# Three blocks of 2048 channels on one core: attention heads with split weight units, the bias table's place in the queue, and norms from sums of the last product

## The reference

```python
# block 1: a convolution, gated linear attention, attention over a memory (4 heads)
x = x + y @ w_out;  x = rmsnorm(x, final_g)
# block 2
h = rms_norm(x, norm1_g);  q, k, v, qi, ki, wi, u_s, v_s, ga, gb = split(h @ w_in)
attn = sparse_attention(...)     # 16 heads, top-64 mask, relative bias rel_bias
x = x + (sigmoid(ga) * attn + sigmoid(gb) * sgu) @ w_out
x = x + square(relu(rms_norm(x, norm2_g) @ w_ff1)) @ w_ff2;  x = rms_norm(x, final_g_2)
# block 3
h = rms_norm_3(x, g_pre);  out = (gated MLA attention, 8 heads, and an RWKV scan)(h) @ w_out
x = x + rms_norm_3(out, g_post)
# rmsnorm(x, g) = x * rsqrt(mean(x*x over channels) + 1e-6) * g
```

## Time and profile before

| | |
|---|---|
| median of 3 runs | 4388.12 us (4385.96 to 4388.28) |
| the profiled execution's own time | 4383.17 us |
| its span | 4381.4 us |
| granted TensorE clock, mean | 0.956 |
| TensorE busy | 3999.8 us (91%) |
| VectorE busy | 2473.3 us (56%) |
| ScalarE busy | 1763.0 us (40%) |
| DMA queue of SP | 634.65 MB, 41.9% of 16 engines |

### The profile page before, as it was taken

How to read it: one execution, slowest core, us unless ns; L and a number is a source line. 1 busy time by engine, 2 the same in 40 slices (tenths; PEclk the granted TensorE clock), 3 DMA queues, 4 the chain that set the end, 5 groups by cost and what they waited for, 6 DMA issues and landing times. The chain is left out here.

```text
span 4381.4 us, 87595 instructions
## 1 busy us (share of the span) xinstructions
PE 3999.8 (91%) x36434; PEld 3884.3 (89%) x36434; DVE 2473.3 (56%) x3418; ACT 1763.0 (40%) x2232; POOL 0.2 (0%) x4
## 2 busy tenths in 40 slices
PE   7999989989898899787799999999899899988898
PEld 7999989889888899776798999999899788888788
DVE  4788765965545544435555555454546655565454
ACT  3434343344444433333344444343344333344543
POOL 0000000000000000000000000000000000000000
PEclk9999999999999998898899999999999999999999
DMA  4545444335444453423354555555554211134343
GB/s 178 173 169 183 154 141 158 112 128 179 148 154 154 160 183 127 153 77 136 115 192 155 182 183 182 183 182 183 171 181 145 107 41 41 41 111 130 137 164 135
DMA packets 99246, 638.54 MB, mean 146 GB/s; under 512 B 11136, under 2 KB 14592, under 8 KB 28224
## 3 DMA queue, kind: packets, MB, share of 16 engines
q1 hardware_dynamic: 98976, 634.65, 41.9%
HBM read 626.18 MB, written 8.42 MB: 145 GB/s over the span
## 5 line engine op out<-in xcount | busy, mean ns | idle before, releaser
L252 PE MATMUL ps_gemm<-arena_r,w_hi 128*128 128x256 f32 x16576 | 2224.3, 287 | 117.9 <-ACT w_hi L193 57.2
L252 PEld LDWEIGHTS ps_gemm<-arena_r,w_hi 128*128 128x128 f32 x16576 | 2107.6, 195 | 139.4 <-issue 72.6
L199 DVE TENSOR_TENSOR ring_r<-ring,w_hi 128x1024 fp32r<-128x1024 f32 (+3 forms) x1264 | 1416.4, 1125 | 1206.7 <-ACT w_hi L193 1194.2
L193 ACT ACTIVATE w_hi<-ring 128x1024 fp32r<-128x1024 f32 (+3 forms) x1264 | 1229.2, 978 | 1323.1 <-PE ps_gemm L252 1061.2
L252 PE MATMUL ps_gemm<-arena_r,ring_r 128*128 128x256 f32 x8288 | 1197.4, 286 | 47.5 <-DVE ring_r L199 46.7
L252 PEld LDWEIGHTS ps_gemm<-arena_r,ring_r 128*128 128x128 f32 x8288 | 1086.9, 194 | 58.1 <-DVE ring_r L199 55.5
L249 PE MATMUL ps_gemm<-w_hi,arena_r 128*128 128x256 f32 (+1 forms) x1408 | 193.3, 288 | 1.0 <-ACT w_hi L193 0.9
L1051 DVE SCALAR_TENSOR_TENSOR arena<-arena,vecs (+15 forms) x480 | 192.1, 462 | 0.0
L249 PEld LDWEIGHTS ps_gemm<-w_hi,arena_r 128*128 128x128 f32 x1408 | 183.0, 198 | 3.0 <-ACT w_hi L193 1.9
L394 ACT ACTIVATE arena<-ps_gemm 128x512 f32 (+2 forms) x99 | 59.1, 597 | 247.9 <-PE ps_gemm L252 190.7
L415 ACT ACTIVATE act_tmp<-ps_gemm 128x512 f32<-128x512 f32 x70 | 41.7, 596 | 158.2 <-PE ps_gemm L252 158.1
(11 more groups left out here) (311 smaller groups left out, 2345.7 us busy)
## 6 DMA issues: line engine op xcount, KB each, us to landing
ring<-in_ff SPq DMA_DIRECT2D x128, 1024.0 KB, 5.2
ring<-in_w_out SPq DMA_DIRECT2D x48, 1024.0 KB, 5.1
ring<-in_gate SPq DMA_DIRECT2D x32, 1024.0 KB, 5.0
ring<-in_conv_a SPq DMA_DIRECT2D x16, 1024.0 KB, 5.1
ring<-in_conv_b SPq DMA_DIRECT2D x16, 1024.0 KB, 5.0
ring<-in_gla_v SPq DMA_DIRECT2D x16, 1024.0 KB, 5.0
ring<-in_conv_z SPq DMA_DIRECT2D x16, 1024.0 KB, 5.0
ring<-in_conv_out SPq DMA_DIRECT2D x16, 1024.0 KB, 5.0
```

The lines of the kernel that those rows point to most:

```text
L193: nc.scalar.activation(w_hi[q % 2][:, 0:size], ring[slot][:, part], ACT.Copy).then_inc(hi_ready, 1)
L199: nc.vector.tensor_tensor(ring_lo[slot][:, part], ring[slot][:, part], w_hi[q % 2][:, 0:size].bitcast(F32), ALU.subtract).then_inc(lo_read ...
L252: mm = nc.tensor.matmul(bank[0:cw, 0:T], w[:, k * cols + c * cw:k * cols + (c + 1) * cw], r[:, kk, :], start=start, stop=stop)
```

## The change

Four edits. (1) `attention`: the quarters of the side product are spread over half heads (`cut`): TensorE does one share before the transposes and one between them and the output product; ScalarE and VectorE follow by parts; on VectorE the output of the head before, then the next maximum, come after the scaling and before the remainders. (2) In the top-k stage SP issues the bias copies before the weight loads. (3) The last product of blocks 1 and 2 also sums squares weighted with the squared gain (`gain`), so both norms' sums are known; `norm_twice` makes both roots from them and multiplies by the product of both gains in one step. The inner norm's `mid` is made from unit 2 to 5 of the first product. (4) In `norm_twice` SP runs the stage's loads first, then stores `mid`.

```diff
@@ Prod.pe, Prod.dve_split, Prod.dve (when sums is set)
-                    for c in range(2):
-                        mm = nc.tensor.matmul(psa[:, 0, 0:T], ones[:, :], stat[:, c, :], start=c == 0, stop=c == 1)
+                    for k in range(2 if s.gain else 1):
+                        for c in range(2):
+                            mm = nc.tensor.matmul(psa[:, k, 0:T], ones[:, :], stat[:, 2 * k + c, :], start=c == 0, stop=c == 1)
...
+                    if s.gain:
+                        for c in range(2):
+                            k = 2 * i2 + (2 * j + c)
+                            nc.vector.scalar_tensor_tensor(out=stat[:, 2 + c, :], in0=s.sums[:, bass.ds(k, 1), :].rearrange("p a t -> p (a t)"),
+                                                           scalar=small[:, bass.ds(k + 40, 1)], in1=stat[:, 2 + c, :], op0=ALU.mult, op1=ALU.add)
                     nc.vector.tensor_tensor(total, total, s.chunks(s.sums, i2, j), ALU.add).then_inc(squares_added, 1)
...
+                    if s.gain:
+                        g = vecs[:, VEC_AT[s.gain]:VEC_AT[s.gain] + DC]
+                        nc.vector.tensor_tensor(small[:, 40:40 + DC], g, g, ALU.mult)
+                        nc.vector.memset(stat[:, 2:4, :], 0.0)
@@ norm_twice
+            def make(dve, q):
+                for c in range(4 * q, 4 * q + 4):
+                    x = nc.vector.scalar_tensor_tensor(out=dst[:, c, :], in0=src[:, c, :], scalar=both[:, c:c + 1], in1=outer, op0=ALU.mult, op1=ALU.mult)
+                return x
...
                 def _(sp):
+                    run.sp(sp)
                     for q in range(4):
                         sp.wait_ge(normed, b_norm + q + 1)
                         sp.dma_start(spill[:, 4 * q:4 * q + 4, :], mid[:, 4 * q:4 * q + 4, :]).then_inc(spilled, 16)
-                    run.sp(sp)
                     sp.wait_ge(spilled, 64)
...
-                    root(act, b_in + 1)
-                    for q in range(4):
-                        act.wait_ge(normed, b_norm + q + 1)
-                        nc.scalar.activation(scratch[:, 4 * q:4 * q + 4, :], mid[:, 4 * q:4 * q + 4, :], ACT.Square).then_inc(sq_ready, 1)
-                    root(act, b_in + 2)
+                    root(act, b_in + 1, outer)
                     parts.act(act)
+                    root(act, b_in + 2, inner)
                     run.act(act)
...
-                    for c in range(DC):
-                        pe.wait_ge(sq_ready, b_sq + c // 4 + 1)
-                        mm = nc.tensor.matmul(psa[:, 1, 0:T], ones[:, :], scratch[:, c, :], start=c == 0, stop=c == DC - 1)
...
+                    link(v.tensor_tensor(both, vecs[:, VEC_AT[gain1]:VEC_AT[gain1] + DC], vecs[:, VEC_AT[gain2]:VEC_AT[gain2] + DC], ALU.mult))
+                    dve.wait_ge(sums_done, b_sums)
+                    link(v.tensor_scalar(inner, psa[:, 0, 0:T], 1.0 / D, EPS, ALU.mult, ALU.add))
+                    link(v.tensor_scalar(stat[:, 2, :], inner, EPS, None, ALU.mult))
+                    v.scalar_tensor_tensor(out=outer, in0=psa[:, 1, 0:T], scalar=1.0 / D, in1=stat[:, 2, :], op0=ALU.mult, op1=ALU.add).then_inc(root_in, 2)
+                    dve.wait_ge(root_done, b_root + 1)
+                    link(v.reciprocal(outer, outer))
+                    parts.dve(dve)
+                    lead.dve_unit(dve, 0)
+                    dve.wait_ge(root_done, b_root + 2)
+                    link(v.reciprocal(inner, inner))
+                    lead.dve_unit(dve, 1)
+                    for u in range(2, lead.n):
+                        if u < 6:
+                            for c in range(4 * u - 8, 4 * u - 4):
+                                x = v.scalar_tensor_tensor(out=mid[:, c, :], in0=src[:, c, :], scalar=vcol(gain1, c), in1=inner, op0=ALU.mult, op1=ALU.mult)
                             x.then_inc(normed, 1)
-                    parts.dve(dve)
-                    run.dve(dve)
+                        lead.dve_unit(dve, u)
@@ attention (pe, dve, act)
-            share = [range(h * m // nh, (h + 1) * m // nh) for h in range(nh)]
+            cut = [4 * m * h // (2 * nh) for h in range(2 * nh + 1)]
+            def beside(quarter, eng, h, half):
+                for n in range(cut[2 * h + half], cut[2 * h + half + 1]):
+                    quarter(eng, n // 4, n % 4)
...
-                        for u in share[h]:
-                            side.pe_unit(pe, u)
+                        if side:
+                            beside(side.pe_quarter, pe, h, 0)
                         pe.wait_ge(p_done, h + 1)
...
                         mm.then_inc(tr_done, 1)
+                        if side:
+                            beside(side.pe_quarter, pe, h, 1)
                         pe.wait_ge(trc_done, h + 1)
...
                     for h in range(nh):
-                        if h + 1 < nh:
-                            maximum(h + 1)
                         b = 8 + 4 * (h % 2)
...
                         x.then_inc(p_done, 1)
-                        for u in share[h]:
-                            side.dve_unit(dve, u)
-                        dve.wait_ge(o_done, h + 1)
...
                         if h:
+                            output(h - 1)
+                        if h + 1 < nh:
+                            maximum(h + 1)
+                        for half in range(2 if side else 0):
+                            beside(side.dve_part, dve, h, half)
+                        if gate is not None and h:
                             remainder(h - 1)
+                    output(nh - 1)
...
-                        for u in share[h]:
-                            side.act_unit(act, u)
+                        if side:
+                            beside(side.act_part, act, h, 0)
                         act.wait_ge(tr_done, h + 1)
...
+                        if side:
+                            beside(side.act_part, act, h, 1)
@@ sparse_attention, sync engine
-                    side.sp(sp)
                     sp.wait_ge(act_b, 1)
...
                         sp.dma_start(RBv[k], src).then_inc(dma_b, 16)
+                    side.sp(sp)
                     sp.wait_ge(dma_b, 48)
```

More of the change, by code:

```diff
@@ L231, in pe_body, with body @@
             r_hi, r_lo = rhs
-            def body(i2, j):
+            def body(i2, j, quarters=range(4)):
                 slot = (g0 + j) % 2
-                pe.wait_ge(bank_free, i2 + (g0 + j + 1))
-                for q in range(4):
+                if 0 in quarters:
+                    pe.wait_ge(bank_free, i2 + (g0 + j + 1))
+                for q in quarters:
                     ring_slot, part, _, n = quarter_of(g0 + j, q)
@@ L266, in build, with __init__ @@
         class Prod:
-            def __init__(s, name, rhs, kind, dst=None, src=None, bias=None, scale=1.0, natural=False, at=0, after=False, rows=P, step=2, split=None, needs_loads=False, sums=None, also=None, before=None):
+            def __init__(s, name, rhs, kind, dst=None, src=None, bias=None, scale=1.0, natural=False, at=0, after=False, rows=P, step=2, split=None, needs_loads=False, sums=None, also=None, before=None, gain=None):
                 s.g0 = st.unit
@@ L802, in layer_norm_silu, with norm_twice @@
             counts(4, 1, 1, 1 + side.n, count[0], side.n)
-        def norm_twice(src, gain1, mid, spill, dst, gain2, scratch, split, then, **kw):
+        def norm_twice(src, gain1, mid, spill, dst, gain2, split, then, **kw):
             _, b_sums, b_in, b_root, b_chain, b_norm = norm_base
-            b_sq = norm_base[0]
             count = [0]
-            parts = make_split(mid, dst, DC, gain2, split)
+            both = small[:, 0:DC]
+            inner, outer = stat[:, 1, :], stat[:, 3, :]
+            def make(dve, q):
+                for c in range(4 * q, 4 * q + 4):
+                    x = nc.vector.scalar_tensor_tensor(out=dst[:, c, :], in0=src[:, c, :], scalar=both[:, c:c + 1], in1=outer, op0=ALU.mult, op1=ALU.mult)
+                return x
+            part = lambda buf: (lambda q: buf[:, 4 * q:4 * q + 4, :])
+            parts = Split(4, make, part(dst), part(split[0]), part(split[1]))
             run = Run(*then, **kw)
-            run.prods[0].fresh = by_quarter(parts.split0 + 4, 4)
+            lead = run.prods[0]
+            lead.fresh = by_quarter(parts.split0 + 4, 4)
             (spilled,) = stage_sems("spilled")
@@ L957, in _, with output @@
                             link(nc.vector.tensor_tensor(x, x, sig, ALU.mult))
+                    def output(h):
+                        dve.wait_ge(o_done, h + 1)
+                        if gate is None:
+                            nc.vector.tensor_copy(o(h), psa[:, 3, 0:T]).then_inc(oc_done, 1)
+                        else:
+                            nc.vector.tensor_tensor(o(h), psa[:, 3, 0:T], gate[2](h), ALU.mult).then_inc(oc_done, 1)
                     for h in range(nh):
[L959 to L960 removed]
                         b = 8 + 4 * (h % 2)
@@ L1115, in block_1 @@
```

(4 more changed lines are left out.)

22 lines of the change are left out of this document (8 added, 14 removed).

## The result

The changed kernel takes **4269.23 us** (median of 4 runs, 4265.84 to 4271.06) against 4387.25 (4385.96 to 4388.28) for the kernel before on the same chip: a ratio of 0.973, 95% interval 0.9713 to 0.9747. The profiled execution took 4270.07 us, its span 4268.3.

A forecast was written before the change was run, and what follows sets the result against it. TensorE was taken to set the end almost everywhere, gains lying where it stands still. Terms -53 -10.2 -13.9 -12.9 -24.9 +16.0 = -98.9 us gave 4284 from the profiled 4383.17, 4289 against the median 4388.12; range 4270 to 4312.

The forecast's parts named there:

- Attention, block 2: Block 2's attention stage: quarters around the transposes remove both waits, 9.2 us a head, 151 against 204 us, 53 us less.
- the bound of 57: Block 2's attention: the most it could gain, 57 us, if the overlap of pieces counted end to end is full.
- Blocks 1 and 3: Attention of blocks 1 and 3: the copy's wait goes, 10.2 us (7 to 12) and 13.9 us (11 to 15) less.
- Bias order: End of the top-k stage: bias copies leave earlier, so TensorE starts 12.9 us sooner (12 to 13.2).
- Norms and stores: Between blocks, twice: shorter norm chains give 24.9 us (22 to 27), late-landing residual stores cost 16.0 (8.6 to 18.6).
- my two ends for the stores: Ends of the block entries: stores land 4.3 us late if sharing without loss, 9.3 us late if in a row.
- nearer the second, but the fixed part once: Ends of the block entries: stores nearly in a row with loads, fixed part counted once, 8.0 us late each.
- the free stores (1): Ends of the block entries: the stores cost nothing, 115 us less in all, 4273 us; 9 in 100.
- the unfilled halves (2): Attention: about 1.4 us of the copy's wait stays in each of 28 heads, +39, 4328 us; 8 in 100.
- the queue of VectorE's remainders (3): Attention: remainders behind two TensorE waits make every half pay 2.5 us, +140, slower at 4429 us; 2 in 100.
- the unchanged order (4): Attention: new loops leave TensorE's order as it is, the norms alone changed, 22 us less, 4366 us; 1 in 100.
- all the marks named for the forecast: Profile after: even heads, clock over 0.95, norm 11 to 13 us, no copy or bias waits, two 10 to 12 us waits.

The follow-up runs named there:

- e12: The changed kernel run once more, unaltered, on another chip: 4269.22 us.
- e1: The changed kernel with the attention loop of before (whole units, VectorE's old order), the rest as changed: 4358.08 us.
- e2: The changed kernel with SP's bias copies behind the weight loads again: 4288.33 us.
- e3: The changed kernel with the two norms between blocks, the sums and the place of the residual's stores as before: 4288.76 us.
- e4: The changed kernel with SP issuing the residual's four stores right after the weight loads of the block's first product: 4257.18 us.
- e5: The changed kernel with the residual's four stores issued from GpSimd's own queue as each quarter is made: 4257.77 us.
- e10: The changed kernel with the residual's stores right after the lead product's loads in block 3 only, last in block 2: 4259.97 us.
- e11: The kernel before with one edit, SP issuing the residual's stores after all loads of the stage: 4405.79 us against 4386.53.
- e13 to e15: The changed kernel with an added stage of 2, 5 or 8 VectorE clears ahead of the RWKV stage: 4271.68, 4271.34 and 4277.52 us.
- e7: The changed kernel with the same quarters per head, but all ahead of the transposes and none after: 4320.7 us.
- e9: The changed kernel with the residual's stores right after the lead product's loads in block 2 only, last in block 3: 4260.3 us.

## Why the prediction was wrong, step by step

Against the profiled execution the forecast was 98.9 us less, and 113.1 came. Two steps failed: the forecast put the stages that the change does not touch at nothing, without a reason, and they gave 10.1 us; and its head of block 2's attention was 0.44 us too long, which made that term 6.1 us too small. Either alone would have left the time inside the range. The missing 14.2 is 10.1 and 6.1, 0.3 each for block 3's attention and the bias order, 0.5 for norms and stores, 1.8 for the last stretch, less 5.0 at the start. With the stretches of the table:

- **Untouched stages: nothing forecast, 10.1 measured** (RWKV stage 7.9, the one before it 2.2). **This is the larger of the two steps that failed.** The forecast had no term for it and its range no room: I took stages that keep their code to keep their time. What decides between about 409 and 417 us was settled in part. Shown: the changed kernel has 409 in both of its profiles (e12); attention does not bring it about (e1); undoing the bias order or the norms takes it away (e2, e3), and so does moving the stores in both blocks (e4, e5). Some 4.6 to 4.8 us of the difference lie in the first 100 us and go with the places of the low clock stretches there; in the changed kernel one of them falls ahead of the wait for VectorE and costs nothing. The rest, 0.8 to 3.4 us, and all 4.1 us of e10, come later, with a stop of TensorE of 1 to 2 us and with further low stretches. Open is what puts a kernel into one form or the other, and what makes the stop. The pause at block 3's entry alone does not decide it (e11), nor does a start up to 6 us later (e13 to e15).
- **Attention, block 2: 53 forecast, 59.1 measured. This is the other step that failed.** The mechanism was right (idle time gone, clock 0.99, no wait left), the term was mis-sized. I put a head together as 0.60 + 2.86 + 5.76 = 9.2 us; it takes 8.78. From the start of one piece to the next it is 0.36 for the transposes, 2.95 and 3.07 for the quarters and 2.40 for the output product and scores. The 2.86 ran to the modelled end of the last scores, 1856.05, though a TensorE record's end lies beyond the start of the next: in e7, after the same wait, the next quarter starts 2.50 us after the output product (1833.63 to 1836.13). The transposes were 0.24 us too long in the same way and the quarters 0.26 too short. So 0.44 us too much in 16 heads, 7 us, less 1 us because 4.4 us of the stage's 144.9 lie outside the 16 heads and not 3.5. I had named the overlap, as the bound of 57, and even that was short.
- **Blocks 1 and 3: 10.2 and 13.9 forecast, 10.2 and 14.2 measured** (e1: 9.9 and 14.3). e7, which takes away nothing there but the cover behind the transposes, gives 9.9 and 15.6 back.
- **Bias order: 12.9 forecast, 13.2 measured**, and 13.2 again in e2. Its weight loads behind the copies cost nothing, as said.
- **Norms and stores: 24.9 - 16.0 forecast, 9.4 net measured for 8.9.** From the sum product on, the chains gave 12.6 and 13.1 us (12.45 each forecast). The forecast's chain starts one step earlier and counts the two multiply-adds, which are there (3.43 us ahead of the sum product for 2.64); like for like it is 11.8 and 12.3. The items of its chain also add up to 11.3 us and not to the 11.5 it states. The stage ends lost 9.2 and 8.9 (8.0 each). Of my two ends for the stores, sharing without loss (4.3) and in a row (9.3), the second was right; "nearer the second, but the fixed part once" was 1 us too kind. The estimate from the Trainium skill's page "DMA: Bandwidth & Descriptors", "Anatomy of one DMA", 6.9 us, was further off. e11 gives the stores' term alone: 19.3 us. That the net fits all the same is in part luck: the products of block 2's entry, from the first to the last load, took 184.2 us for 187.2, at a granted clock of 0.96 for 0.95, and no term foresaw these 3.0 us.
- **The start: 5.0 us against the change**, the last stretch 1.8 for it (with the attention loop of before, e1, it takes 165.9 us again). The stage ahead of block 1's attention took 135.3 us in the profile of before and 138.5 in that of every other kernel, e11 among them, whose code is the same to there. So 3.2 of the 5.0 us are that execution, which was a quick one; the forecast allowed for this by setting its 98.9 against the median, which lay 4.95 us higher. With the 0.84 us by which the profiled run after lies above its median this closes the account: 14.2 + 4.95 + 0.84 = 20.0 us, the distance from 4289 to 4269.2 but for rounding.

Of the rivals, the free stores (1) are refuted by the two idle rows of 12 us and by e11; the unfilled halves (2), the queue of VectorE's remainders (3) and the unchanged order (4) by the even 8.78 us. Rival 1's time, 4273, was nearer than mine for a wrong reason.

What would have shown it wrong: all the marks named for the forecast are there but for details (heads 8.8 us apart in block 2, 13.7 in block 1 and 15.3 in block 3, a clock over 0.95, 11.4 and 11.0 us for the norm, two waits of 11.9 and 12.2 us, where 10 to 12 was named). No mark was named for the size of the head, or for the stages outside.

**A better kernel than both** came out: with the stores behind the lead product's loads (e4) 4257.2 us, or from GpSimd's queue (e5) 4257.8, 12 us under the changed kernel; by e9 and e10 the edit in one block alone gives 9.

## What to carry to other kernels

Measure a piece of TensorE's work from its start to the start of the next, never to the end of its record; over 16 heads the difference was 7 us. To cover a small copy between two dependent products, put work on both sides of it, and spread the work evenly first: in block 2 the even spread was worth 31 us, the cover 21.5, and the order of the other engine 6 alone and nothing in the end. A store issued behind the last loads of a stage made the stage end 9 us later here; issue it once its data are ready, ahead of loads that have lead, or on another queue.

## What was not expected of the hardware

- An unchanged stage took 409 to 417 us in 17 profiles. A low stretch of TensorE's clock that fell ahead of a wait for VectorE cost nothing; where all of them fell behind it, 4.6 to 4.8 us were lost in the first 100; and a stop of TensorE of 1 to 2 us that nothing in the profile explains came with every time of 413 us or more. The changed kernel kept its form in its two profiles (409.0 and 409.2). The Trainium skill, "TensorE: Matmul & The Clock Gate", "Part 1", has the chip watch TensorE's activity on a clock of its own that does not start with the work. The traces agree in this: the same 3.37 us of idle time ahead of the stage are followed by a low stretch at 1.4 us in the changed kernel, and by none before 12.0 us in e2. The length of the stage is explained by it only in part.
- Parts of a change did not add up: undone one by one they cost 89 + 19 + 19.5 = 127.5 us, together 118; the moved stores gave 9 and 9 us alone and 12 together. More than half of the gap is this one stage: e2 and e3 lose 5.5 and 8.1 us in it, the change gained 7.9 there once. Below 10 us the verdict on one edit here needs the stage's own time, not the kernel's.
